# Root for x's scaling in a PSUM bank, the last 80 projection columns in one product, keys doubled later, the second head's scores ahead of turning the second tokens

## The reference, cut to what matters

```python
return rmsnorm(x, final_g)                       # end of the first block
...
proj = h @ w_in[l]                               # second block: 5200 columns
p_pool, p_q, p_k, p_v, p_qi, p_ki, p_wi = split_columns(proj)
...                                              # p_ki: 64 columns, p_wi: 16 columns
rel = jax.nn.relu(jnp.einsum('bqhd,bsd->bqhs', qi, k_idx))
score = jnp.einsum('bqh,bqhs->bqs', wi, rel).astype(jnp.float32) * INDEXER_SCALE
_, sel = lax.top_k(score, top_k)
...
h = layer_norm(ALPHA * h + mix, ln1_g[l], ln1_b[l])
qh = (xc @ wq).reshape(PEER_CHUNK, PEER_HEADS, 2, PEER_HALF)    # peer_ffn
s1 = jnp.einsum('thd,kd->thk', qh[:, :, 0], sub_keys[0])
s2 = jnp.einsum('thd,kd->thk', qh[:, :, 1], sub_keys[1])
...                                              # top 16 of each, then of the 256 sums
u_sel = u[expert]                                # 128 gathered rows of u per token
act = jax.nn.gelu(jnp.einsum('td,thkd->thk', xc, u_sel))
```

## Time and profile before

| | us |
|---|---|
| median of 3 runs | 2827.48 (2821.9 to 2834.83) |
| the profiled execution: its own time | 2820.8 |
| its span | 2818.9 |
| PE busy | 2222.1 (79%) |
| POOL busy | 2048.5 (73%) |
| DVE busy | 2015.0 (71%) |
| ACT busy | 1246.6 (44%) |

### The profile page before, as it was taken

The page is one execution under the profiler, slowest core; times in us unless marked ns, Lnnn a source line. Parts: engine busy times, 40 slices in busy tenths (PEclk is TensorE's granted clock), DMA queues, the critical chain, the costliest instruction groups (busy, mean ns, idle before and its releaser), DMA issues.

```text
span 2818.9 us, 40877 instructions
## 1 busy us (share of the span) xinstructions
PE 2222.1 (79%) x12632; PEld 1959.1 (69%) x12632; DVE 2015.0 (71%) x3006; ACT 1246.6 (44%) x2130; POOL 2048.5 (73%) x1148
## 2 busy tenths in 40 slices
PE   7997999999999999999998811003334499999997
PEld 7996888888888888899987710002323378887785
DVE  4998652724426258465448999999998889888887
ACT  5435355454454544233531000008987754444443
POOL 4775878989889887587763566787686657777774
PEclk9999999999999999999999965555555599999998
DMA  7552555555555555364446999999899869999996
GB/s 224 166 162 77 192 164 179 192 180 194 192 188 187 186 186 181 111 210 150 162 154 241 411 380 370 385 418 377 349 413 378 343 235 341 323 321 316 317 321 253
DMA packets 232081, 713.84 MB, mean 253 GB/s; under 512 B 17420, under 2 KB 53828, under 8 KB 198848
## 3 DMA queue, kind: packets, MB, share of 16 engines
q1 hardware_dynamic: 168512, 364.08, 38.1%
q0 software_dynamic: 57344, 343.97, 31.2%
q10 hardware_dynamic: 6144, 4.81, 0.6%
HBM read 709.12 MB, written 3.67 MB: 253 GB/s over the span
## 4 chain that ended last, share of the span: by engine, by line
PE 35%; POOL 22%; DVE 19%; issue 18%; DMA 2%; ACT 1%; POOLq 1%; DVEq 1%; ACTq 0%; another core or an unknown queue 0%
PE bank L539 15%; PE bank L541 8%; POOL vrows L503 8%; POOL w_lo L423 5%; DVE rows_split L1991 5%; DVE rows_act L1991 3%; PE bank L544 3%; PE bank L545 3%; PE bank L546 3%; POOL rows_split L486 2%; DVE misc L1676 2%; POOL vring L497 2%; DVE rows_raw L1991 1%; PE bank L870 1%; POOL rows_split L458 1%
## 5 line engine op out<-in xcount | busy, mean ns | idle before, releaser
L423 POOL TENSOR_TENSOR w_lo<-raw,w_hi 128x1024 fp32r<-128x1024 f32 x464 | 1133.3, 2463 | 309.9 <-ACT w_hi L1043 309.2
L1043 ACT CAST w_hi<-raw 128x1024 fp32r<-128x1024 f32 x464 | 483.5, 1050 | 644.0 <-PE bank L541 409.9
L539 PE MATMUL bank<-B,w_hi 128*128 128x512 f32 x1280 | 452.0, 396 | 19.9 <-POOL w_lo L423 8.7
L539 PE MATMUL bank<-A,w_hi 128*128 128x512 f32 x1280 | 446.3, 393 | 3.7 <-DVE X L1705 2.1
L503 POOL DMA_INDIRECT vrows<-in_peer_v,vring x256 | 336.2, 1313 | 146.7 <-POOL vring L497 99.3
L541 PE MATMUL bank<-B,w_lo 128*128 128x256 f32 x1280 | 360.7, 282 | 0.0
L541 PE MATMUL bank<-A,w_lo 128*128 128x256 f32 x1280 | 357.9, 280 | 0.0
L544 PE MATMUL bank<-A,w_hi 128*128 128x256 f32 x1152 | 332.8, 289 | 12.0 <-DVE proj L1758 5.7
L1714 DVE TENSOR_TENSOR sq<-bank,T 128x256 f32<-128x256 f32 x128 | 53.5, 424 | 396.3 <-ACT T L1212 396.3
L545 PE MATMUL bank<-A,w_hi 128*128 128x256 f32 x1152 | 328.8, 285 | 0.0
L546 PE MATMUL bank<-A,w_lo 128*128 128x256 f32 x1152 | 328.7, 285 | 0.0
(11 more groups left out here) (315 smaller groups left out, 4874.8 us busy)
## 6 DMA issues: line engine op xcount, KB each, us to landing
raw<-in_mlp_w SPq DMA_DIRECT2D x128, 1024.0 KB, 5.2
v_raw<-in_peer_v SPq DMA_DIRECT2D x128, 736.0 KB
raw<-in_w_in SPq DMA_DIRECT2D x40, 1024.0 KB, 5.0
raw<-in_cc_w_in SPq DMA_DIRECT2D x64, 512.0 KB, 4.7
raw<-in_cc_w_out SPq DMA_DIRECT2D x16, 1024.0 KB, 5.0
raw<-in_w_out SPq DMA_DIRECT2D x16, 1024.0 KB, 5.1
raw<-in_peer_wq SPq DMA_DIRECT2D x16, 1024.0 KB, 19.1
vrows<-in_peer_v,vring POOLq DMA_INDIRECT x256
```

The costliest lines, as they stand in the source:

```text
L423: nc.gpsimd.tensor_tensor(w_lo[:, s % 4], raw[:, s // 2, 2 * (s % 2):2 * (s % 2) + 2, :], w_hi[:, s % 4].bitcast(F32), ALU.subtract).then_ ...
L539: nc.tensor.matmul(bank[m][:].rearrange("p (s t) -> p s t", s=2), wh, both[:, :, kt, :], start=(kt == 0), stop=False)
L1043: nc.scalar.copy(w_hi[:, s % 4], raw[:, s // 2, 2 * (s % 2):2 * (s % 2) + 2, :]).then_inc(hi_done, 1)
```

## The change

Four things. DVE copies `rstd` into PSUM bank `misc3` and scales x with that copy. The 80 columns are loaded without the gap and multiplied in one series of 16 products of 80 columns against 256 tokens; ACT copies the 80x256 result to SBUF (`kw`). At step 2 of project(2) a new function `keys_and_heads` doubles the keys by a product with two identity matrices side by side (`twice`) and turns the 16 head-weight rows by two transposes; ACT then copies the doubled keys and DVE takes the head weights. ACT rounds step 3 of project(2) between its two copies. In the query stage the second head's scores come before `tokens_turned(4)`, for PE and for ACT; banks `misc2` and `misc3` are then waited for before the transposes reuse them.

```diff
-        wt = at("wt", o_z + 48 * KB, [P, KT, 144])
+        wt = at("wt", o_z + 48 * KB, [P, KT, IDX_DIM + IDX_HEADS])
+        twice = at("twice", o_z + 54 * KB, [IDX_DIM, 2, IDX_DIM])
+        kw = at("kw", o_z + 55 * KB, [IDX_DIM + IDX_HEADS, TOK])
...
             def tail_columns():
+                pe.wait_ge(wt_in, 64)
+                pe.wait_ge(n_out["rms3"], 2 * KT)
+                n = IDX_DIM + IDX_HEADS
+                for k in range(KT):
+                    last = nc.tensor.matmul(misc[0][0:n, 0:TOK], wt[:, k, :], X[:, k, :], start=(k == 0), stop=(k == KT - 1))
+                last.then_inc(tail_ps, 1)
+
+            def keys_and_heads():
+
                 pe.wait_ge(wt2_ok, 1)
-                pe.wait_ge(n_out["rms3"], 2 * KT)
-                for k in range(KT):
-                    nc.tensor.matmul(misc[0][:, 0:TOK], wt[:, k, 0:P], X[:, k, :], start=(k == 0), stop=(k == KT - 1))
+                pe.wait_ge(tail_ok, 1)
+                n = IDX_DIM + IDX_HEADS
+                nc.tensor.matmul(misc[2][:, 0:TOK], twice[:].rearrange("p b n -> p (b n)"), kw[0:IDX_DIM, :], start=True,
+                                 stop=True)
                 for t in range(NT):
-                    for k in range(KT):
-                        last = nc.tensor.matmul(misc[1][:, t * 16:t * 16 + 16], X[:, k, t * P:(t + 1) * P],
-                                                wt[:, k, P:P + 16], start=(k == 0), stop=(k == KT - 1))
+                    last = nc.tensor.transpose(misc[1][:, t * P:t * P + n], kw[:, t * P:(t + 1) * P], ident[0:n, 0:n])
                 last.then_inc(tail_ps, 1)
...
-            project(2, {1: tail_columns, 3: first_scores})
+            project(2, {1: tail_columns, 2: keys_and_heads, 3: first_scores})
...
                     if r >= 4:
                         pe.wait_ge(hn_ok, r - 3)
+                    if r >= 6:
+                        pe.wait_ge(key_ok, SCORED.index((r - 6, 0, 1)) + 1)
...
             first_queries(3)
+            second_head()
             tokens_turned(4)
-            queries(G_QRY + 1, {0: second_head})
+            queries(G_QRY + 1, {})
...
             def keys_twice():
-                act.wait_ge(wt_in, 64)
-                nc.scalar.copy(wt[:, :, 0:64], wt[:, :, 64:128]).then_inc(wt2_ok, 1)
+                nc.scalar.copy(twice[:], ident[0:IDX_DIM, 0:IDX_DIM].unsqueeze(1).broadcast_to([IDX_DIM, 2, IDX_DIM])
+                               ).then_inc(wt2_ok, 1)
 
             def tail():
                 act.wait_ge(tail_ps, 1)
+                nc.scalar.copy(kw[:], misc[0][0:IDX_DIM + IDX_HEADS, 0:TOK]).then_inc(tail_ok, 1)
+                round_sub(G_PROJ + 2, 3, landed(G_PROJ + 2))
+                act.wait_ge(tail_ps, 2)
                 act.wait_ge(n_op["rms3"], KT)
-                nc.scalar.copy(kidx[:], misc[0][:, 0:TOK]).then_inc(tail_ok, 1)
-                nc.scalar.mul(widx[:], misc[1][:, 0:32].rearrange("p (t h) -> p t h", t=NT), IDX_SCALE
-                              ).then_inc(tail_ok, 1)
+                nc.scalar.copy(kidx[:], misc[2][:, 0:TOK]).then_inc(tail_ok, 1)
...
             query_out(0, 3)
+            head_scores(1)
             tokens_out(4)
-            head_scores(1)
...
             reciprocal_root("rms3", misc[0], RMS_EPS, n_mean["rms3"])
+            step(V.tensor_copy(misc[3][:, 0:TOK], rstd[:]))
             read_out(0)
             for k in range(KT):
-                V.scalar_tensor_tensor(X[:, k, :], X[:, k, :], VT[:, V_FIN + k:V_FIN + k + 1], rstd[:],
+                V.scalar_tensor_tensor(X[:, k, :], X[:, k, :], VT[:, V_FIN + k:V_FIN + k + 1], misc[3][:, 0:TOK],
                                        ALU.mult, ALU.mult).then_inc(n_out["rms3"], 1)
             step(V.memset(pbuf[:], 0.0))
             read_out(1)
-            dve.wait_ge(tail_ok, 2)
+            dve.wait_ge(tail_ps, 2)
+            V.tensor_scalar(widx[:], misc[1][:, 0:TOK].rearrange("p (t n) -> p t n", t=NT)[:, :, IDX_DIM:IDX_DIM + IDX_HEADS],
+                            IDX_SCALE, None, ALU.mult).then_inc(tail_ok, 1)
+            dve.wait_ge(tail_ok, 3)
```

More of the change, by code:

```diff
@@ L690, in tail_columns @@
             def tail_columns():
+                pe.wait_ge(wt_in, 64)
[5 more added lines that the diff above has]
+            def keys_and_heads():
                 pe.wait_ge(wt2_ok, 1)
-                pe.wait_ge(n_out["rms3"], 2 * KT)
-                for k in range(KT):
-                    nc.tensor.matmul(misc[0][:, 0:TOK], wt[:, k, 0:P], X[:, k, :], start=(k == 0), stop=(k == KT - 1))
+                pe.wait_ge(tail_ok, 1)
+                n = IDX_DIM + IDX_HEADS
+                nc.tensor.matmul(misc[2][:, 0:TOK], twice[:].rearrange("p b n -> p (b n)"), kw[0:IDX_DIM, :], start=True,
+                                 stop=True)
                 for t in range(NT):
-                    for k in range(KT):
-                        last = nc.tensor.matmul(misc[1][:, t * 16:t * 16 + 16], X[:, k, t * P:(t + 1) * P],
-                                                wt[:, k, P:P + 16], start=(k == 0), stop=(k == KT - 1))
+                    last = nc.tensor.transpose(misc[1][:, t * P:t * P + n], kw[:, t * P:(t + 1) * P], ident[0:n, 0:n])
                 last.then_inc(tail_ps, 1)
             def first_scores():
-                pe.wait_ge(tail_ok, 2)
+                pe.wait_ge(tail_ok, 3)
                 pe.wait_ge(proj_ok, 8)
                 index_scores(1, list(same_rows(0, 8, 2)))
-            project(2, {1: tail_columns, 3: first_scores})
+            project(2, {1: tail_columns, 2: keys_and_heads, 3: first_scores})
             pe.wait_ge(idx_acc, 8)
@@ L847, in second_head @@
                 pe.wait_ge(bank_free[3], G_QRY + 2)
-                pe.wait_ge(hn_ok, 8)
+                pe.wait_ge(hn_ok, 4)
                 for t in range(NT):
@@ L855, in work @@
                     pe.wait_ge(bank_free[3], G_QRY + g + 2)
+                    pe.wait_ge(hn_ok, 8)
                     if g != 2:
@@ L1254, in small_weights @@
                 for p in range(4):
-                    act.dma_start(wt[:, 4 * p:4 * p + 4, 64:144], w2[:, 4 * p:4 * p + 4, 5120:5200]).then_inc(wt_in, 16)
+                    act.dma_start(wt[:, 4 * p:4 * p + 4, :], w2[:, 4 * p:4 * p + 4, 5120:5200]).then_inc(wt_in, 16)
             def mixer_tables():
@@ L1312, in _ @@
                 G = G_PROJ + i
-                ahead(G, landed(G), landed(G + 1), middle=middles.get(i), first=3 if i else MORE)
+                ahead(G, landed(G), landed(G + 1), middle=middles.get(i), first={0: MORE, 2: 4}.get(i, 3))
                 if i in after:
```

## The result

The changed kernel takes 2804.86 us (median of 10 runs, 2791.55 to 2811.75), the kernel before, measured beside it, 2822.18 (10 runs, 2810.61 to 2834.83). The ratio is 0.9926, 95% interval [0.9907, 0.9945]: between 15.5 and 26.2 us faster. Run again twice, each time beside the kernel before, it gave 0.991 [0.9878, 0.9942] and 0.9948 [0.9934, 0.9962]. The profiled execution took 2796.54 us, its span is 2794.7.

What follows compares the result with a forecast made beforehand. PE was held ahead of project(2) by DVE, whose SBUF scalings of x waited for POOL. Projection -15.9 and second head +0.7 make -15.2 us, from 2827.48 to 2812.3; forecast's own range 2809.5 to 2816.5, wider range 2802 to 2821.

Steps and rivals of the forecast that it cites:

- The projection: From project(1)'s end to project(3)'s scores: wait, second series and slow PE go, copy and doubling come; 49.8 to 33.9, -15.9 us.
- B: Rival: the copy of the root waits for one POOL operation, +2.5, sum -12.7, 2814.8 us; chance 0.08.
- C: Rival: the load of the 80-column weights is not hidden, +6, sum -9.2, 2818.3 us; chance 0.07.
- D: Rival: the scalings of x still wait for POOL and PE's gap stays, sum -8.0, 2819.5 us; chance 0.05.
- The term for slow PE: Project(2)'s eight steps, slow around the wait and the 16-column series, go from 26.8 to 23.5 us: -3.3.
- a drop of the clock stays: Caveat on project(2)'s steps: if PE's clock still drops, up to half of the -3.3 us is not gained.
- The second head: Query stage: earlier scores save 5.0 us at first, but delayed weight chunks make choose(0,1) later: +0.7 us, bounds -5.0 and +3.9.
- rival A: The second head's 5 us stay, as PE starts the second query group earlier and requests chunks earlier; 2806.6 us, chance 0.14.
- The bound from the Trainium skill's rule of turns: DMA engines serve queues packet by packet in turn, so the second head is worth at most the slack of 1.4 us.
- E: Rival, slower: query weights starve behind the gathers, 11 us for each MB ahead; sum +4.7, 2832 us, chance 0.03.
- The level: Starting time of the kernel before, taken as the median of the runs, 2827.48 us, from which the forecast was stepped.

Runs made afterwards that it cites:

- e1: The kernel before with only the root copied to a PSUM bank and x scaled with that copy; 0.9969.
- e2: The kernel before with only the 80 columns in one series and the keys doubled at step 2 of project(2); 0.9952.
- e3_head: The kernel before with only the second head's scores moved ahead of turning the second tokens; 0.9981.
- e6: The changed kernel with the root copied to another SBUF tile instead of the PSUM bank; 2815.76 us in a single run.
- e4_no_head: The changed kernel with the second head's scores put back behind the transposes; 0.9942.
- after_third: The changed kernel itself, run again on one chip with other kernels; 0.9948 against the kernel before.
- after_again: The changed kernel itself, run again beside its three parts on the same chip; 0.991 against the kernel before.
- e7: The changed kernel with half of each weight chunk of query groups 2 to 4 loaded on ACT's DMA queue instead of SP's; 0.9948.
- e8: The changed kernel with rms2's and rms3's running sum of squares, the squared root and the scaled hidden-layer products in PSUM; 2793.53 us, 0.9896.
- e9: e8 with the product for rms3's mean of squares at step 4 of project(0) instead of step 7; 0.9904.

## Why the prediction was right, and where it was not

**The projection** was right. Forecast 49.8 to 33.9 us, -15.9; measured -16.2 in the profiled pair. PE's wait went, nothing took its place, the copy cost 0.43 (forecast 0.45), the 80-column series 6.91 as with 128 columns, doubling and turning 0.92 in two rows (forecast 1.0). Rivals B, C and D are out by these rows and by e1 and e2.

**The term for slow PE** was mis-sized, and its cause half told. I took -3.3 and bound it to "the wait and the series" together. e1 and e2 part them: 1.6 us belong to the standstill, 1.9 to the series in before's own trace and 3.7 in e3_head's, which is the same code. Against that trace the projection gained 18.4 us, not 16.2. The fear that "a drop of the clock stays" was idle: B is 30.3 in every trace with the new series but e6's, 30.7, where the clock stayed at 0.50 from PE's restart at 1152.0 to the series and was 0.94 in it.

**The second head** is the step that failed in its mechanism: "which delays the next weight chunks by 2 us", with `choose(0,1)` 0.7 us later than before. The bytes were missing, 0.18 MB at first and 0.46 by the time of the scores. But the chunks already asked for slipped by 0.35 to 0.42 us, not 2, and the one that the scores wait for by 0.04, and that one was asked for 5.1 us earlier. So `choose(0,1)` came 1.3 us earlier, which is the slack of the earlier trace rows, and a wait of 3.77 us stands where I had 5 to 6. My fault was to turn bytes of a queue into the landing of one chunk at a fixed rate, and to leave out that PE's earlier start moves the request: rival A named that, and I gave it no term in the sum. The bound from the Trainium skill's rule of turns (DMA: Bandwidth & Descriptors, "Queues, rings and completion order"), at most the slack of 1.4 us, which I weighed beside it, holds. And then 0.8 of the 1.3 us went to rows that came later: the term is -0.5 against before's trace, not +0.7, and nothing against e4_no_head's. Rival A's early request was real, but its 5 us are out (D2 would be 5 us shorter), and E never began.

**The level** is the larger miss in number. I started from the median of three runs, 2827.48. Ten runs beside the changed kernel have 2822.18. Of the 7.4 us by which the forecast of 2812.3 lies above 2804.86, 5.3 are this, and 2.1 the size of the change (-15.2 against -17.3 in the medians). The first ratio means -20.9 and the third -14.7 us; the traces account for 16.7 to 18.9 us (16.2 to 18.4 in the projection, 0.5 for the second head). The rest I put down to the scatter of unchanged code shown below; the runs don't divide it further. The larger misses, the level, the second head and the slow PE, all lie on one side; none of them made up for another.

## What to carry to other kernels

Where DVE falls behind beside a busy GpSimd, look for operations with both tensors in SBUF that last as long as GpSimd's, and give them one operand, or a running sum, in a free PSUM bank: it took 16 scalings from 26.1 to 6.4 us and, done for the sums and the scaled products too, another 14 us off the kernel (0.9948 to 0.9896 on one chip). Price a series of products with the clock it leaves behind: the 16-column one took 8.4 us and cost 1.9 to 3.7 more. Before moving work to fill a wait, find out whether the DMA engines set the time of the stage: here the new order won no more than the slack at the next stop, and kept less than half of it. And when work moves forward, ask which requests move with it, not only which bytes.

## What the runs showed of the hardware that was not expected

- The executions of unchanged code differ in pace. Between 500 and 1000 us, where PE is never idle, the 512-column product took 391 ns on the mean in before and in two of the changed kernel's three traces (the first and after_third), 399 in e1_root, e2_tail, e3_head and after_again, at clock 1.00 in each; e7 and e8 have 394. PE gets 2% fewer products done in those 500 us. It isn't the chip: e4_no_head has 399 on the chip on which after_third and e9 have 391. Here before and e3_head, by line (busy us, mean ns, idle before):

```profile
L539 PE MATMUL bank<-A,w_hi 128*128 128x512 f32 x768 | 266.4, 391 | 0.0
```

```profile
L539 PE MATMUL bank<-A,w_hi 128*128 128x512 f32 x738 | 260.9, 399 | 0.0
```

  The reciprocal of the root, the first mark of the projection, so lies anywhere from 1108 to 1128 us in kernels that are equal up to there. What sets the pace isn't settled; the 1.2 us lost between projection and query stage look like the same thing in the mixer's groups (22.5 us each in the changed kernel's first trace, 22.1 in before and in its other two).
- A single-tensor copy inside SBUF took as long as a GpSimd operation too (2.32 us in e6), not only operations on two SBUF tensors, as the first paragraph of the prediction has it. The reciprocal just ahead of it, from SBUF to SBUF too, took 1.75 us in every trace.
- 32 products with 16 moving columns, 64 passes, bring the clock down although PE is busy without a gap (e1_root: 1.00 before, 0.70 in the series, 0.50 behind it).
